# Hybrid decoder trunk on one core: S5 set-up, preparation and steps placed unit by unit in three projections

## What is computed

```python
for l in range(DEPTH):
    h = rmsnorm(x, norm_mix[l])
    proj = h @ w_in[l]
    (u, dq, dk, dv, iq, ik, iw, rq, rk, rv, rg) = jnp.split(proj, split_pts, axis=-1)
    y_a = s5_mixer(u, ...)            # diagonal state space model, 16 groups of 64 states, and a gate (glu)
    y_b = dsa_attention(dq, dk, dv, iq, ik, iw, rel_bias)   # 256 best keys of each query by an indexer's score
    y_c = retention(rq, rk, rv, rg, ret_gn[l])              # chunks of 128, rotary positions, group norm
    x = x + jnp.concatenate([y_a, y_b, y_c], axis=-1) @ w_out[l]
    h = rmsnorm(x, norm_ffn[l])
    gate, up = jnp.split(h @ w_ffn_in[l], 2, axis=-1)
    x = x + (jax.nn.silu(gate) * up) @ w_ffn_out[l]
```

## Time and profile before

| | us |
|---|---|
| median of 3 runs | 2755.93 (2754.32 to 2762.28) |
| the profiled execution | 2759.82, span 2757.9 |

### The profile page before, as it was taken

One profiled execution on the slowest core, in us unless ns is written; L12 is line 12 of the kernel. 1 busy time (PEld: TensorE's weight loads), 2 busy tenths in 40 slices (PEclk: granted clock), 3 DMA queues, 4 the chain that ended last, 5 costly groups with the idle time before them and its releaser, 6 DMA issues. The chain is left out here.

```text
span 2757.9 us, 34637 instructions
## 1 busy us (share of the span) xinstructions
PE 2586.0 (94%) x13515; PEld 2032.9 (74%) x13515; DVE 1546.3 (56%) x2691; ACT 1017.9 (37%) x1478; POOL 1309.6 (47%) x818
## 2 busy tenths in 40 slices
PE   8887889989999999999999989998999999999998
PEld 6666666667777787777777767766777778888887
DVE  3857567688999225644331386477899942211111
ACT  5222244334344433324344412442525354322222
POOL 3332145445454474545555522443646346555654
PEclk9988999999999999999999999999999999999999
DMA  5231113122222144323322331221222215333332
GB/s 160 74 117 50 39 32 107 54 69 70 76 73 72 49 160 117 88 60 97 90 75 79 90 120 54 69 69 54 77 69 74 65 54 177 95 95 101 101 118 86
DMA packets 385665, 232.90 MB, mean 84 GB/s; under 512 B 29592, under 2 KB 371552, under 8 KB 383072
## 3 DMA queue, kind: packets, MB, share of 16 engines
q1 hardware_dynamic: 385136, 229.62, 28.0%
q10 hardware_dynamic: 368, 1.08, 0.1%
HBM read 213.88 MB, written 14.69 MB: 83 GB/s over the span
## 5 line engine op out<-in xcount | busy, mean ns | idle before, releaser
L693 POOL TENSOR_TENSOR w_lo<-w_raw,w_hi 128x1024 fp32r<-128x1024 f32 (+2 forms) x408 | 900.5, 2208 | 1299.6 <-ACT w_hi L804 1299.6
L1727 PE MATMUL psum<-h_hi,w_hi 128*128 128x512 f32 x1984 | 801.8, 404 | 23.5 <-ACT h_hi L828 7.0
L804 ACT ACTIVATE w_hi<-w_raw 128x1024 fp32r<-128x1024 f32 (+2 forms) x408 | 397.3, 974 | 1087.7 <-PE psum L1727 1048.4
L1727 PE MATMUL psum<-h_lo,w_hi 128*128 128x512 f32 x1984 | 770.3, 395 | 0.9 <-POOL h_lo L701 0.9
L1727 PE MATMUL psum<-h_hi,w_lo 128*128 128x512 f32 x1984 | 515.3, 391 | 0.0
L1727 PEld LDWEIGHTS psum<-h_hi,w_hi 128*128 128x128 f32 x1984 | 378.1, 191 | 137.3 <-issue 41.4
L1727 PEld LDWEIGHTS psum<-h_lo,w_hi 128*128 128x128 f32 x1984 | 378.3, 191 | 79.6 <-issue 2.2
L1727 PEld LDWEIGHTS psum<-h_hi,w_lo 128*128 128x128 f32 x1984 | 374.1, 189 | 76.5
L1328 DVE MAX8 top<-scores 128x8 f32<-128x512 f32 (+5 forms) x352 | 324.1, 921 | 6.5
L1330 DVE MATCH_REPLACE8 scores<-top,scores 128x512 f32<-128x512 f32 (+5 forms) x352 | 319.0, 906 | 0.0
L1727 PE MATMUL psum<-a_hi,w_hi 128*128 128x512 f32 x704 | 286.3, 407 | 18.5 <-ACT w_hi L804 8.3
(11 more groups left out here) (308 smaller groups left out, 2951.3 us busy)
## 6 DMA issues: line engine op xcount, KB each, us to landing
w_raw<-in_w_ffn_in_dram SPq DMA_DIRECT2D x176, 512.0 KB, 3.9
w_raw<-in_w_ffn_out_dram SPq DMA_DIRECT2D x96, 384.0 KB, 3.1
w_raw<-in_w_in_dram SPq DMA_DIRECT2D x68, 512.0 KB, 3.7
w_raw<-in_w_out_dram SPq DMA_DIRECT2D x32, 512.0 KB, 3.6
x_half<-xs SPq DMA_DIRECT2D x8, 1024.0 KB, 6.7
xs<-x_half SPq DMA_DIRECT2D x8, 1024.0 KB, 6.3
w_raw<-in_w_ffn_out_dram SPq DMA_DIRECT2D x32, 256.0 KB, 2.7
out_dram<-mixed SPq DMA_DIRECT2D x8, 512.0 KB, 3.6
```

The source lines that it names most:

```text
L693: eng.tensor_tensor(w_lo(u, n), w_raw[:, u % 3, 0:n], w_hi[:, u % 2, 0:n].bitcast(F32), ALU.subtract).then_inc(sems["weights_ready"], 1)
L804: act(w_hi[:, u % 2, 0:n], w_raw[:, u % 3, 0:n], ACTF.Copy).then_inc(sems["hi_ready"], 1)
L1727: return eng.matmul(out_, lhsT, rhs, start=start, stop=stop, skip_group_check=True)
```

## The change

A new function `place(main, *behind)` puts given lists of side steps behind given units; it takes the place of `weave` in three projections. In the first projection of layer 0, set-up steps 3 and 4 move from behind units 7 and 8 to behind units 10 and 12, scores 3 and 4 come one and two units earlier, block 2's rounds begin behind unit 9 as before but are cut in other portions, and the eight rounds of block 3 that stood there move to the second projection. In that one the retention steps, the preparations and S5's steps get units of their own: S5 begins behind unit 4 in place of 7, three steps of it no longer stand together, block 3's rounds begin behind unit 4, and S5's steps 14 and 15 move behind unit 14, ahead of the attention. In layer 1, preparations 0 and 1 move to the end of the first projection, and in the second S5 starts behind unit 1 in place of 4, with preparations 2 to 5 between its steps.

For that, preparations 4 and 5 get another temporary place (`Xt` in scratch in place of `prep_tmp`, which lies over `Kt`), and DVE waits for its own last instruction at the end of S5's steps 5 and 12.

```diff
--- before.py
+++ after.py
@@ -88,6 +88,14 @@
     return out + side[n:]
 
 
+def place(main, *behind):
+
+    out = []
+    for n, unit in enumerate(main):
+        out += [unit] + (behind[n] if n < len(behind) else [])
+    return out
+
+
 def blend(steps, others):
 
     out, n = [], 0
@@ -148,10 +156,9 @@
     side = [("boot", t) for t in range(TT + 1, NB + 2)] + [("bias", s) for s in range(3)]
     out += weave(main[:4], blend(param_steps(0), side)) + main[4:5] + [("rstd", "boot"), ("diag",)]
     sc = score_steps(0, 0)
-    out += main[5:6] + [("s5_set", 0, 0), ("s5_set", 0, 1)]
-    for n in range(3):
-        out += main[6 + n:7 + n] + [sc[n], ("s5_set", 0, 2 + n)]
-    out += weave(main[9:15], rounds(2, 0, 4) + sc[3:4] + rounds(2, 4, 10) + sc[4:] + rounds(2, 10) + rounds(3, 0, 8))
+    setup = [("s5_set", 0, s) for s in range(5)]
+    out += place(main[5:15], setup[:2], [sc[0], setup[2]], sc[1:2], sc[2:3], sc[3:4] + rounds(2, 0, 2),
+                 sc[4:] + setup[3:4], rounds(2, 2, 6), setup[4:] + rounds(2, 6, 8), rounds(2, 8, 12), rounds(2, 12))
     out += main[15:16] + [("spread", "fill")] + retention_steps(0, 0, 0, 2) + main[16:17]
     out += retention_steps(0, 0, 2, 3) + main[17:18]
     drain = main[18:]
@@ -159,11 +166,16 @@
     out += [("fillnorm", "xa", 0, main[0][-1], "tmp")] + drain
     out += [("dma", "store_x1_first", main[0][-1]), ("dma", "load_bias", 0), ("dma", "store_x0", 0)]
     s5 = [("s5", 0, s) for s in range(16)]
-    ret = blend(retention_steps(0, 0, 3), [("s5_prep", 0, n) for n in range(6)])
-    out += weave(main[:14], blend(ret + s5, rounds(3, 8, 16)), 0)
+    ret = retention_steps(0, 0)
+    prep = [("s5_prep", 0, n) for n in range(6)]
+    three = rounds(3)
+    out += place(main[:14], ret[3:5] + prep[:1], ret[5:7] + prep[1:2], ret[7:9] + prep[2:3], ret[9:11] + prep[3:4],
+                 ret[11:12] + s5[:1] + three[:2], ret[12:13] + s5[1:2] + three[2:4], ret[13:] + s5[2:3] + three[4:5],
+                 s5[3:4] + prep[4:5] + three[5:6], s5[4:6] + prep[5:], s5[6:7] + three[6:8], s5[7:9] + three[8:9],
+                 s5[9:11], s5[11:13] + three[9:10], s5[13:14] + three[10:12])
     att = [attend_steps(0, 0, b) for b in range(TT)]
-    side = blend(att[0] + att[1] + att[2], rounds(3, 16)) + att[3] + [("attend_end", 0, 0, s) for s in range(2)]
-    out += weave(main[14:], side, 0, 6)
+    side = blend(att[0] + att[1] + att[2], three[12:]) + att[3] + [("attend_end", 0, 0, s) for s in range(2)]
+    out += weave(main[14:], s5[14:] + side, 0, 6)
     out += [("dma", "load_x0", 0)]
 
     def late(l):
@@ -204,7 +216,8 @@
     out += weave(main[:8], side + [("s5_set", 1, s) for s in range(5)])
     sc = score_steps(1, 0)
     out += weave(main[8:15], sc[:3] + blend(rounds(2, 0, 12), sc[3:])) + main[15:16] + [("spread", "fill")]
-    out += weave(main[16:18], rounds(2, 12))
+    prep = [("s5_prep", 1, n) for n in range(6)]
+    out += weave(main[16:18], rounds(2, 12) + prep[:2])
     ffn = window("ffn", 0, 1)
     out += [("fillnorm", "xs", DEPTH, ffn[0][-1], "tmp")] + main[18:]
     side = blend(retention_steps(1, 0), rounds(3, 0, 16)) + attend_steps(1, 0, 0)
@@ -216,7 +229,10 @@
 
     main = window("proj", 1, 1)
     out += [("sums", "inside")] + main[:1] + scales() + [("dma", "swap_x", main[0][-1])]
-    out += weave(main[1:N_PROJ], [("s5_prep", 1, n) for n in range(6)] + [("s5", 1, s) for s in range(16)], 0, 15)
+    s5 = [("s5", 1, s) for s in range(16)]
+    out += place(main[1:N_PROJ], s5[:1] + prep[2:3], s5[1:2] + prep[3:4], s5[2:3], s5[3:4], s5[4:5] + prep[4:5],
+                 s5[5:6] + prep[5:], s5[6:7], s5[7:9], s5[9:10], s5[10:11], s5[11:12], s5[12:13], s5[13:14], s5[14:15],
+                 s5[15:])
     out += [("fillmix", 1, 0, counter[0])] + main[N_PROJ:]
 
     out += mix_and_ffn(1, 0, *late(1))
@@ -1550,9 +1566,9 @@
                     cmul(Et[:, 0, :, n:2 * n], Et[:, 1, :, n:2 * n], Et[:, 0, :, 0:n], Et[:, 1, :, 0:n],
                          rr, ri, *t_)
 
-            def inputs(g, c):
-
-                za, zb = (prep_tmp[:, i, :].rearrange("p (m q e) -> p m q e", m=8, q=4) for i in range(2))
+            def inputs(g, c, place):
+
+                za, zb = (place[:, i, :].rearrange("p (m q e) -> p m q e", m=8, q=4) for i in range(2))
                 of_g = slice(4 * g, 4 * g + 4)
                 pr, pi = (pw[i][:, 0:8, of_g].unsqueeze(3).broadcast_to(zs) for i in range(2))
                 tt(za, pr, s5_bb[:, c, of_g, :].unsqueeze(1).broadcast_to(zs), MUL)
@@ -1573,14 +1589,14 @@
                 if n == 0 and l == 0:
                     eng.wait_ge(sems["x1_stored"], 16)
                 if n < 2:
-                    inputs(0, n)
+                    inputs(0, n, prep_tmp)
                 elif n == 2:
                     first_rotation()
                     rotations(0, 0, 5, prep_tmp)
                 elif n == 3:
                     rotations(0, 5, 7, prep_tmp)
                 else:
-                    inputs(1, n - 4)
+                    inputs(1, n - 4, Xt)
 
             def s5(l, s):
                 if s == 15:
@@ -1654,6 +1670,7 @@
                     tt(fa, er, hi, MUL)
                     link(tt(fb, ei, hr, MUL))
                     tt(Gt[:, 1, :, 1:P], x4[0], x4[1], ADD).then_inc(sems["hprev_ready"], 1)
+                    eng.wait_ge(sems["hprev_ready"], st.add("hprev_ready"))
 
             def final(h, t):
                 if not 1 <= t <= TT:
```

## The result

| kernel | median, us | spread | ratio to before (95% interval) |
|---|---|---|---|
| before | 2759.02 | 2754.32 to 2762.28 | |
| changed | 2711.86 | 2706.09 to 2715.17 | 0.9828 (0.9802 to 0.9854) |

The account below looks back on a forecast made before the run. PE's work, plus 172 us standing still and half-clock losses, was taken to bound the kernel, with DVE late in the changed stretches. Gains 5 + 13 + 0 + 18 = 36 from 2755.9 gave 2720 us, range 2704 to 2742.

Parts of the forecast that it names:

- First projection, the mechanism: Layer 0's first projection: PE's 8.6 us stop at unit 10 goes, a new one of some 8 us comes at unit 15.
- Its size: First projection's gain: 5 us, rotated keys at 143.5 instead of 148.4; bounds 0 to 15.4.
- still one for L1397: First projection: PE still waits for the rotation at L1397, with the rotation 5 us earlier.
- stays DVE-bound: First projection: it was bound by DVE and stays so, gaining 5 us.
- Second projection, what goes: Layer 0's second projection: PE's stops of 13.7, 6.6 and 1.5 us, smaller waits and half clock go, 30 us.
- What comes for ACT: Second projection, new waits for ACT: root 3.6 us plus 1.5 half clock, S5 step 2 1.1, gate 4 plus 1 clock.
- The lateness of DVE, 6 us: Second projection: DVE reaches three meeting points with PE 0 to 5 us late, 6 in sum; about five more products blocked.
- Layer 1: Layer 1: moved preparations cost 0, at most 3; its second projection gains 18 us, 15 idle and 3 half clock, bounds 10 to 19.
- The second (DVE as the bound, 2733): Rival: DVE becomes the bound of the second projection, which gives 0, all else holds: 2733; chance 0.25.
- The first (full release, 2708, a gain of 48): Rival: contention misses S5, ACT's root comes in time; second projection 20 to 24, first 6 to 8: 2708; chance 0.17.
- The third (slower): Rival: second projection keeps its stops, eight rounds add 12 us and blocked products 24: 2769; chance 0.05.
- the fourth (no effect): Rival: stops only change places in all three projections: 2756; chance 0.03.

Follow-up runs that it names:

- layer 1 undone: Changed kernel with layer 1 as before the change, its preparations and S5 steps woven over the second projection again: 2730.2 us, 0.9898.
- preparations back: Changed kernel with layer 1's preparations 0 and 1 back at the start of its second projection, behind unit 0: 2720.24 us, 0.9858.
- gate: Changed kernel with projection unit 15 placed between S5's gate and the first attention in layer 0: 2708.48 us, 0.9815.
- zeros: Changed kernel with POOL writing zeros in place of its weight subtraction for ten units around the second projection's units 3 to 12: 2707.73 us, 0.9813.
- retention 11 first: Changed kernel with retention 11 ahead of preparation 3 on DVE, in place of behind it: 2710.48 us, 0.9824.
- rounds later: Changed kernel with four of the eight block-3 rounds ahead of the second projection's unit 10 moved behind it: 2709.09 us, 0.9819.
- layer 1 woven: Changed kernel with layer 1's preparations 2 to 5 and S5 steps woven as before, preparations 0 and 1 still moved: 2720.98 us, 0.9873.
- the pair: Changed kernel with set-up 4 cut, plus retention 11 ahead of preparation 3 and five block-3 rounds moved behind unit 10: 2694.92 us, 0.9768.

## Why the prediction was right, and where its terms were off

- **Direction, range and order of the stages: right.** 2711.86 lies in 2704 to 2742, though just outside the forecast's own 2712 to 2728, and all three stages gave more than forecast. The three stages were forecast at 5, 13 and 18 and came at 10.2, 20.5 and 19.9 in the profiles; undoing the first gave 9 and the third 19, which leaves 19 for the second.
- **First projection, the mechanism: right.** The stop at unit 10 went, and one of "some 8 us" came at unit 15: 7.9, with the copies at 124.24 where I had 126. **Its size: half.** The rotated keys are there at 139.9, not 143.5. Of the 3.6 us, 1.2 are the earlier start and 1.8 the retention's steps 0 to 2, which I had priced at 11.0 from an execution in which the first product, L1390, took 3.08 us; after, it took 1.22, and one of the six was held up in place of two:

```profile
130.71 1.22 DVE L1406 TENSOR_TENSOR scratch<-scratch,cst 128x1024 f32<-128x1024 f32 x1
...
135.49 3.31 DVE L1412 TENSOR_TENSOR scratch<-scratch 128x1024 f32<-128x1024 f32 x1
```

  And I said "still one for L1397". In the profiled execution PE had just come, with no wait left. But in four other profiles with this order of the first projection (layer 1 undone, preparations back, gate, zeros) it did wait 1.5 to 1.6 us for it: there unit 15 took 7.1 to 7.2 us in place of 8.55, and units 5 to 18 the same 92.2 to 92.6 us in sum. So the rotation sets this stage's end, as I had written, and what unit 15 lost more to half clock cost nothing. The larger miss is that I gave the vanished wait no half clock. Before, PE came out of it at half clock; from the end of the rotation to unit 18 it needed 10.4 us, after 7.5 (before, then after):

```profile
148.40:158.80 10.40, 10.32 (x41) 9.00 (x42) 6.07 (x11) 3.85 (x7) 3.84 (x3) 0.71 0.00 0
...
139.90:147.40 7.50, 7.48 (x42) 6.45 (x42) 6.01 (x9) 4.86 (x8) 5.46 (x4) 1.00 0.26 70
```

  These 2.9 us, the 1.8 and small ones make the 5 I was short. That the first projection "stays DVE-bound" was right of the order as it stood, and cutting set-up 4 showed that it wasn't a bound of the stage.
- **Second projection, what goes: right.** All of 13.7, 6.6 and 1.5 us went.
- **What comes for ACT: right.** For L993 3.0 with 3.6 forecast, for L1077 1.3 with 1.1. At the gate it is 5.2, but a stop of 1.9 had stood there before, with half clock behind it (that unit took 7.30 us; after, unit 15 took 7.20 for 5.74), so 3.3 over what stood there with 4 forecast, and nothing for the 1 of clock. PE's timeline before:

```profile
344.70 0.47 PE L1727 MATMUL psum<-h_hi,w_hi 128*128 128x512 f32 x1 [1.93 <-ACT scratch L852]
```

- **The lateness of DVE, 6 us: this is the term that failed**, as a number. In the profiled execution it was 0.3. Fewer products were held up than the "about five more" (6 instructions for 9.8 us from 190 to 262 us, against 3 for 6.3 before), and most of that was taken up by DVE's pauses, and it showed at one meeting point only. I had multiplied held-up products by a price without asking which of the three points had slack. As a mechanism it holds: two of the four further profiles of the same order have 4.8 and 5.0 us of lateness around unit 28, each with half clock behind it; with zeros in place of subtractions nothing is held up, and with four rounds fewer 11.3 us of hold-up ahead of the copies bring no stop. So the term belonged in the range (6 too low as a loss in some executions, 6 too high in others), and the forecast of that stage, 13, would have been 19 without it, against 20.5.
- **"Who interferes with whom"** of the Trainium skill's page SBUF — State Buffer says that a DVE instruction with two inputs in SBUF and one of GpSimd that reads SBUF exclude each other for a whole instruction, and that one which only writes doesn't take part. The kernel that only writes on GpSimd agrees: with 0.95 us memsets nothing was held up, with subtractions 9.8 us were. The total that I had worked out without that cost, 2714, was nearer than the 2720 with it: the rule held, and its price was not the sum of the instructions held up, as DVE had pauses.
- **Layer 1: right,** 18 forecast and 19.9 in the trace, with PE idle 0.3 us and a clock of 1.00 over the stage (the third line of the busy times of the result). The move of preparations 0 and 1 cost 0.3 us of a unit in the profile, forecast 0 (at most 3). What I had not seen is how much hung on that move: 8 us.
- **Rivals.** The second (DVE as the bound, 2733) didn't come. It had the right place, unit 28, and a lateness of 5 us in two profiles, but not 13 in any. The first (full release, 2708, a gain of 48) is nearer to the 47 than my forecast of 36, and I had given it 0.17. Its number came by other ways than its reasons: six products were still held up, and ACT's root still cost PE 3.0 us, while its price for the first projection, 6 to 8, was below 10. The third (slower) and the fourth (no effect) didn't come.

## What to carry to other kernels

Look at what stands ahead of a late instruction on its engine, and move what isn't needed there into a pause of that same engine, even if it means cutting a step in two: that was 9 us where the whole stage looked bound. An edit that brings nothing but trades one wait for another is worth a second try together with one that removes the new wait: here the pair went with 7.5 us, though its interplay wasn't tested apart. And a stop of PE can cost more than its length: add the half clock behind it, unless something later sets the stage's end anyway, as the rotation did in the first projection.

## What the hardware showed that I had not expected

- The granted clock after short stops. In the changed kernel PE stood 7.9 us for unit 15 and then ran matmuls of 0.63 us in place of 0.39 to 0.40 (1.2 GHz for 2.4) for some 6 us, which made the unit 8.55 us long for 5.72:

```profile
125.07 0.77 PE L1744 MATMUL psum<-h_hi,w_hi 128*128 128x512 f32 x1 [7.95 <-DVE scratch L1250]
...
130.33 0.63 PE L1744 MATMUL psum<-h_hi,w_hi 128*128 128x512 f32 x1
...
131.18 0.40 PE L1744 MATMUL psum<-h_hi,w_hi 128*128 128x512 f32 x1
```

  The same stretch at half clock stands behind a stop of 4.2 us (unit 224, 6.78 us) and behind one of 3.7 (unit 15 of the second projection, 7.20 us). So between 1 and 3 us were lost each time. It isn't a fixed price: behind the same stop of 7.9 to 8.2 us unit 15 took 8.45 to 8.6 us in four profiles (the changed kernel, retention 11 first, rounds later, layer 1 woven) and 7.1 to 7.2 in four others.
- The same order of work gives a stop or not by 1 to 3 us of shift. Five kernels have the same order up to unit 28; DVE was held up for 7.7 to 9.8 us in three of them and 12.9 and 13.1 in the others, and unit 28 took 6.3 us in the three, 11.33 and 12.75 in the two.
